# Two transformer blocks on one core: the compression product of block one with high and low inputs side by side, and its output product placed behind the first attention score

## The reference, cut to what matters

```python
def compress(kv, pe, w1, w2):
    """Overlapping blocks (length CMP_BLOCK, stride CMP_STRIDE) -> one token via MLP with intra-block pos. emb."""
    B, G, T, dh = kv.shape
    NC = (T - CMP_BLOCK) // CMP_STRIDE + 1
    idx = jnp.arange(NC)[:, None] * CMP_STRIDE + jnp.arange(CMP_BLOCK)[None, :]
    blocks = kv[:, :, idx, :] + pe
    flat = blocks.reshape(B, G, NC, CMP_BLOCK * dh)
    return jax.nn.silu(flat @ w1) @ w2
...
        kc = rmsnorm(compress(heads(kcm, KVH), cmp_pe[i, 0], cmp_w1[i, 0], cmp_w2[i, 0]), nsa_knorm_g[i, 0])
        vc = compress(heads(vcm, KVH), cmp_pe[i, 1], cmp_w1[i, 1], cmp_w2[i, 1])
        s_cmp = jnp.einsum('bgntd,bgcd->bgntc', q_nope, kc) * scale
        p_cmp = masked_softmax(s_cmp, cmp_mask)
        o_cmp = jnp.einsum('bgntc,bgcd->bgntd', p_cmp.astype(vc.dtype), vc)
```

## Time and profile before

| what | value |
|---|---|
| median of 3 runs | 2827.45 us (2824.11 to 2828.16) |
| span of the profiled execution | 2822.0 us |
| between the span and the median of the runs | 5.45 us |
| PE busy | 2731.9 us, 97% of the span |
| DVE, ACT, POOL busy | 1176.7, 1271.7, 1385.1 us |
| mean granted TensorE clock | 0.991 |
| PE of the chain that ended last | 87% |

### The profile page before, as it was taken

The page is one execution under the profiler, slowest core; times in us unless marked ns, Lnnn a source line. Parts: engine busy times, 40 slices in busy tenths (PEclk is TensorE's granted clock), DMA queues, the critical chain, the costliest instruction groups (busy, mean ns, idle before and its releaser), DMA issues.

```text
span 2822.0 us, 41633 instructions
## 1 busy us (share of the span) xinstructions
PE 2731.9 (97%) x13748; PEld 2286.9 (81%) x13748; DVE 1176.7 (42%) x2138; ACT 1271.7 (45%) x2187; POOL 1385.1 (49%) x1713
## 2 busy tenths in 40 slices
PE   8999899999999999999999999999999999999998
PEld 6889668788867878888888888888888788888887
DVE  4768752567775234422242321313442324242232
ACT  5554745655564543545443432424344544343233
POOL 4535444543544454454643655545455464365553
PEclk9999999999899999999999999999999999999999
DMA  5223113322301242233432333334223342233332
GB/s 152 72 51 87 26 31 90 87 72 57 92 9 45 83 113 70 83 102 100 120 98 60 110 100 90 97 97 114 70 82 101 96 125 90 65 107 102 93 97 97
DMA packets 270820, 242.47 MB, mean 86 GB/s; under 512 B 29376, under 2 KB 203648, under 8 KB 270592
## 3 DMA queue, kind: packets, MB, share of 16 engines
q1 hardware_dynamic: 267696, 235.12, 28.7%
q10 hardware_dynamic: 2896, 4.52, 0.5%
HBM read 237.51 MB, written 2.10 MB: 85 GB/s over the span
## 4 chain that ended last, share of the span: by engine, by line
PE 87%; DVE 5%; issue 4%; ACT 3%; POOL 0%; DMA 0%; DVEq 0%; ACTq 0%; POOLq 0%
PE bank L1988 11%; PE bank L1992 11%; PE bank L1991 11%; PE bank L1922 8%; PE bank L1925 8%; PE bank L1926 8%; PE bank L841 5%; PE bank L845 4%; PE bank L844 4%; PE bank L979 2%; PE bank L1877 2%; PE bank L891 1%; PE bank L827 1%; PE bank L894 1%; PE bank L895 1%
## 5 line engine op out<-in xcount | busy, mean ns | idle before, releaser
L2832 POOL TENSOR_TENSOR wlo<-raw,whi 128x256 fp32r<-128x256 f32 (+1 forms) x1616 | 1290.1, 830 | 1302.8 <-ACT whi L2137 1302.5
L2137 ACT CAST whi<-raw 128x1024 fp32r<-128x1024 f32 (+2 forms) x443 | 455.5, 1034 | 598.6 <-PE bank L1988 401.9
L1922 PE MATMUL bank<-xhi,whi 128*128 128x512 f32 x928 | 363.9, 392 | 1.6 <-DVE h L2524 1.6
L1926 PE MATMUL bank<-xhi,wlo 128*128 128x512 f32 x928 | 361.3, 389 | 0.0
L1925 PE MATMUL bank<-xlo,whi 128*128 128x512 f32 x928 | 361.1, 389 | 0.0
L1988 PE MATMUL bank<-whi,xhi 128*128 128x512 f32 x832 | 326.5, 392 | 3.9 <-DVE xlo L2415 3.9
L1992 PE MATMUL bank<-whi,xlo 128*128 128x512 f32 x832 | 324.0, 389 | 0.0
L1991 PE MATMUL bank<-wlo,xhi 128*128 128x512 f32 x832 | 323.8, 389 | 0.0
L841 PE MATMUL bank<-whi,xhi 128*128 128x512 f32 (+2 forms) x672 | 246.6, 367 | 5.5 <-DVE pT L1497 3.1
L844 PE MATMUL bank<-wlo,xhi 128*128 128x512 f32 (+2 forms) x672 | 242.2, 360 | 0.0
L845 PE MATMUL bank<-whi,xlo 128*128 128x512 f32 (+2 forms) x672 | 242.1, 360 | 0.0
(11 more groups left out here) (509 smaller groups left out, 4954.4 us busy)
## 6 DMA issues: line engine op xcount, KB each, us to landing
raw<-in_w_in SPq DMA_DIRECT2D x147, 512.0 KB, 3.7
raw<-in_w SPq DMA_DIRECT2D x132, 512.0 KB, 3.8
raw<-in_w_pg SPq DMA_DIRECT2D x16, 512.0 KB, 3.8
raw<-in_w_o SPq DMA_DIRECT2D x16, 512.0 KB, 3.8
raw<-in_xa_k SPq DMA_DIRECT2D x16, 512.0 KB, 3.9
raw<-in_xa_v SPq DMA_DIRECT2D x16, 512.0 KB, 3.8
raw<-in_xa_q SPq DMA_DIRECT2D x16, 512.0 KB, 4.0
raw<-in_xa_o SPq DMA_DIRECT2D x16, 512.0 KB, 3.8
```

The lines of the kernel that those rows point to most:

```text
L1922: mm = pe.matmul(o, wh, rhs[0][:, k, :], start=(k == 0), stop=False)
L1926: mm = pe.matmul(o, wl, rhs[0][:, k, :], start=False, stop=(k == KD - 1))
L2137: nc.scalar.copy(whi[:, j % SLOTS, 0:nk * cols], raw[:, j % SLOTS, 0:nk * cols]).then_inc(hi_split, 1)
L2832: ins = nc.gpsimd.tensor_tensor(wlo[:, s, part], raw[:, s, part], whi[:, s, part].bitcast(F32), ALU.subtract)
```

## The change

The input of `c_hid` lies as one tensor `chl`, with high and low parts next to each other. One matmul of 124 columns does `whi` by both, and one of 62 columns does `wlo` by the high part: two matmuls in place of three. The two halves of the bank are added by a new DVE reduction to `hsum`, which empties the bank; ACT's sigmoid and DVE's product read `hsum` in place of the bank. In the order, `score 0` and `fill 0` now come first, `c_out` behind them, `nz_exp 1` behind `c_out`, then (by place in the list) `exp 0`, `score 1`, `nz_gate 1`, `fill 1`, `c_key`, `c_score 0`, `score 2`.

```diff
-    s += [("nz_exp", 1), ("c_out",), ("nz_gate", 1)]
     main, last = attention_steps()
-    main.insert(1, ("c_key",))
+    first = [("score", 0), ("fill", 0, FILL[0]), ("c_out",), ("nz_exp", 1)]
+    assert main[:2] == [("score", 0), ("c_score", 0)]
+    main[:2] = first
+    place(main, ("score", 1), [("nz_gate", 1), ("fill", 1), ("c_key",), ("c_score", 0)])
...
-    place(main, ("score", 0), [("fill", 0, FILL[0])], ahead=True)
-    place(main, ("score", 2), [("fill", 1)])
...
+        hsum = Ql[:, 0, 128:128 + 4 * NCMP].rearrange("p (w c) -> p w c", w=2)
...
-            chi0, clo0 = (sb(n, [P, 16, 2, NCMP], F32R, middle) for n in ("chi0", "clo0"))
+            chl0 = sb("chl0", [P, 16, 2, 2 * NCMP], F32R, middle)
...
-                o = G.ps(name)[:, 0:2 * NCMP]
+                both, high = G.ps(name)[:, 0:4 * NCMP], G.ps(name)[:, 0:2 * NCMP]
                 for j in range(8):
-                    a, b = (x[:, 8 * i + j].rearrange("p g c -> p (g c)") for x in ((chi0, clo0), (chi1, clo1))[w])
+                    x = (chl0, chl1)[w][:, 8 * i + j]
                     wh, wl = whi[:, s, j * P:(j + 1) * P], wlo[:, s, j * P:(j + 1) * P]
-                    mm = pe.matmul(o, wh, a, start=(i == 0 and j == 0), stop=False)
+                    mm = pe.matmul(both, wh, x.rearrange("p a c -> p (a c)"), start=(i == 0 and j == 0), stop=False)
                     if j == 0:
                         mm.then_inc(chunk_begun, 1)
-                    pe.matmul(o, wh, b, start=False, stop=False)
-                    mm = pe.matmul(o, wl, a, start=False, stop=(i == 1 and j == 7))
+                    mm = pe.matmul(high, wl, x[:, 0], start=False, stop=(i == 1 and j == 7))
...
             def step_c_hid(step):
                 if step[2] == 1:
-                    gate(("ch", step[1]), 2 * NCMP)
+                    gate(("ch", step[1]), 2 * NCMP, src=hsum[:, step[1], :])
...
             def step_c_hid(step):
                 if step[2] == 1:
-                    name = ("ch", step[1])
+                    name, w = ("ch", step[1]), step[1]
+                    dve.wait_ge(*G.filled(name, l))
+                    nc.vector.tensor_reduce(hsum[:, w, :], G.ps(name)[:, 0:4 * NCMP].rearrange("p (a c) -> p c a", a=2), AX, ALU.add).then_inc(*G.empty(name))
+                    dve.wait_ge(*G.evacuated(name, l))
                     e = et_place()[:, 0:2 * NCMP]
-                    tt_(hid[:, step[1], :], e, G.ps(name)[:, 0:2 * NCMP], ALU.mult).then_inc(*G.empty(name))
+                    tt_(hid[:, w, :], e, hsum[:, w, :], ALU.mult).then_inc(*et_read[0].up())
```

More of the change, by code:

```diff
@@ L587, in build @@
         fa, fb, fc, ft = (tA[:, :], et[:, 0, :]), (tB[:, :], sq[:, 0, :]), (tC[:, :], sq[:, 1, :]), (Ql[:, 0, :], Ql[:, 1, :])
-        chi1 = nc.alloc_sbuf_tensor_at("chi1", [P, 16, 2, NCMP], F32R, offset=decays_at)
-        clo1 = nc.alloc_sbuf_tensor_at("clo1", [P, 16, 2, NCMP], F32R, offset=decays_at + 16 * 2 * NCMP * 4)
+        chl1 = nc.alloc_sbuf_tensor_at("chl1", [P, 16, 2, 2 * NCMP], F32R, offset=decays_at)
         kdt = tC[:, :].rearrange("p (c d) -> p c d", c=TT)
@@ L1061, in step_c_out @@
             def step_c_out(step):
-                for w in range(2):
-                    pe.wait_ge(*G.evacuated(("ch", w), l))
+                gated = [s_ for s_ in steps1[:steps1.index(step)] if s_[0] in ("z_gate", "nz_gate") or s_[0] == "c_hid" and s_[2] == 1]
+                pe.wait_ge(*et_read[0].at(l, len(gated)))
                 pe.wait_ge(*G.free(("co",), l))
@@ L1399, in step_c_in @@
                 act.wait_ge(*G.evacuated(("ct", w, 1), l))
-                nc.scalar.copy((chi0, chi1)[w][:, :, :, :], cin).then_inc(*sigs["hi"].up())
+                nc.scalar.copy((chl0, chl1)[w][:, :, 0, :], cin.rearrange("p j g c -> p j (g c)")).then_inc(*sigs["hi"].up())
             def step_c_hid(step):
                 if step[2] == 1:
-                    gate(("ch", step[1]), 2 * NCMP)
+                    gate(("ch", step[1]), 2 * NCMP, src=hsum[:, step[1], :])
             def step_c_out(step):
@@ L1427, in step_c_turn @@
                 if qt == 0:
-                    act.wait_ge(*et_read[0].at(l, 2 * TT))
+                    act.wait_ge(*et_read[0].at(l, 2 * TT + 2))
                 for g in range(NKV):
@@ L1763, in step_c_in @@
                 dve.wait_ge(*hi_s.next(l))
-                tt_((clo0, clo1)[w][:, :, :, :].rearrange("p j g c -> p (j g c)"), cin.rearrange("p j g c -> p (j g c)"),
-                    (chi0, chi1)[w][:, :, :, :].rearrange("p j g c -> p (j g c)").bitcast(F32), ALU.subtract).then_inc(*clo_ready.up())
+                x = (chl0, chl1)[w]
+                tt_(x[:, :, 1, :], cin.rearrange("p j g c -> p j (g c)"), x[:, :, 0, :].bitcast(F32), ALU.subtract).then_inc(*clo_ready.up())
             def step_c_hid(step):
                 if step[2] == 1:
-                    name = ("ch", step[1])
+                    name, w = ("ch", step[1]), step[1]
+                    dve.wait_ge(*G.filled(name, l))
+                    nc.vector.tensor_reduce(hsum[:, w, :], G.ps(name)[:, 0:4 * NCMP].rearrange("p (a c) -> p c a", a=2), AX, ALU.add).then_inc(*G.empty(name))
+                    dve.wait_ge(*G.evacuated(name, l))
                     e = et_place()[:, 0:2 * NCMP]
-                    tt_(hid[:, step[1], :], e, G.ps(name)[:, 0:2 * NCMP], ALU.mult).then_inc(*G.empty(name))
+                    tt_(hid[:, w, :], e, hsum[:, w, :], ALU.mult).then_inc(*et_read[0].up())
             def step_c_out(step):
```

## The result

The changed kernel takes 2843.22 us (median of 4 runs, 2842.61 to 2845.74), the kernel before on the same chip 2827.8 us (4 runs, 2824.11 to 2829.63). The ratio is 1.0055, with a 95% interval of 1.0043 to 1.0067: 15.4 us slower. That is inside the forecast range of 2832 to 2848 and on the forecast side, 3.7 us above the likeliest value.

A forecast was written before the change was run, and what follows sets the result against it. PE was taken as 87% of the chain, with the attention behind the key copies. Copies later by 5.8 and 6.2 us gave +12.0: span 2822.0 to 2834, median 2827.45 to 2839.5 us, range 2832 to 2848.

The forecast's parts named there:

- The product: Compression product: 64 matmuls a layer instead of 96 save 3.8 us of PE work, all hidden in a wait for DVE.
- rival A: Compression product: the PE work saved reaches the end, with both stalls gone; -12.6 us, 2815; chance 5%.
- The reductions: DVE behind the query rotation: two a layer at 0.28 us, delaying ACT's sigmoids; the subtractions still end at 289.84.
- the cover: ACT's 1.52 us wait for PE before the `qhl` casts hides the sigmoid delay; if gone, up to 1.4 us a layer.
- The stall ahead of the output product: PE after the compression product: `score 0` needs only the last `qhl`, so PE resumes 0.75 and 0.4 us earlier.
- What is late next: `c_out` behind `score 0` and `fill 0` ends at 296.4 in layer one; key copies 6.5 us later, near 302.9.
- The bank: `score 1` shares bank 5 with `c_out` and waits for DVE to read it; worth 1.7 us a layer.
- Rival B: Attention slack absorbs ACT's lateness, so only the stall's 0.75 + 0.4 us are gained; 2826; chance 7%.
- The term that was mis-sized: Second layer's key copies: 780.1 + 6.5 = 786.6 against 780.42, so +6.2 us.
- rival D: Clock falls again behind the new waits, so `score 1` and `fill 1` cost 3.0 us more a layer; +18, 2845; 18%.
- The step from span to time: Whole kernel: the runs' median 2827.45 lies 5.45 us above the profiled span, so span 2834 becomes 2839.5.
- the +12.0: Both layers together: key copies +5.8 us in the first and +6.2 us in the second.

The follow-up runs named there:

- experiment 3: The run of co_bank7: changed kernel with `c_out` in bank 7, `c_key` in 6, `p_turn` in 7 and 4; 2838.09 us.
- order_only: Kernel before with only the lines of the change that set the order, keeping its three-matmul product; 2841.14 us, ratio 1.0047 to before.
- fill1_later: Changed kernel with `fill 1` put back behind `score 2`; 2839.84 us, ratio 1.0041 to the kernel before.
- co_bank7: Changed kernel with `c_out` in bank 7, `c_key` in bank 6, `p_turn` in 7 and 4, set by hand; 2838.09 us, ratio 1.0036 to before.
- co_then_fill: Changed kernel with `c_out` right behind `score 0` and `fill 0` behind it; 2835.86 us, ratio 1.0026 to the kernel before.

## Why the prediction was right, and where a size was off

**The product: right.** I said that PE would be done with the `kk` transposes near 276.8 and wait some 2.7 us for bank 0 behind DVE's rotation; it waits 2.43 and, in the second layer, 5.70. Alone, the product doesn't make the kernel faster (1.0007), which rules out rival A.

**The reductions: right.** Priced at 0.28, they take 0.27 and 0.29. The subtractions `qhl` began at 283.83 and ended at 289.49 (I said 289.84, unchanged). ACT's wait of 1.52 us for PE in the earlier trace rows was the cover, and 0.29 of it is left (283.22).

**The stall ahead of the output product: right in the first layer.** `score 0` at 289.64, forecast 289.9. In the second layer I said 0.4 us gained; there it is a small loss. The rows of DVE's gate product ahead of the stretch, before and changed:

```profile
755.02 0.68 DVE L1606 TENSOR_TENSOR nzs<-nzs,et 128x512 f32<-128x512 f32 x1
```

```profile
760.88 0.68 DVE L1605 TENSOR_TENSOR nzs<-nzs,et 128x512 f32<-128x512 f32 x1
```

The layer starts 5.86 us late. Less that, `score 0` is at 773.24 against the forecast of 772.5, since PE's transposes of `q` ran at the lower clock and ACT had to wait 0.90 us for them; DVE's subtractions began at 773.29 - 5.86 = 767.43, not at 766.8.

**What is late next: right, link by link.** `c_out` ends at 295.9 (forecast 296.4); the wait for bank 5 is 2.12 (2.06); the key copies come at 302.40 (302.9), `exp 1` 5.38 us later (5.26), the wait ahead of `score 4` is 3.14 (some 3). The bank was priced at 1.7 us a layer; experiment 3 gives 1.6 up to the key copies where the clock is the same. That bears out the rule of the Trainium skill that I set against the trace there (Perfetto Trace Analysis, Matmuls: independent groups should rotate through banks): with both groups in bank 5 PE waited 2.12 us in both layers, and with `c_out` in bank 7 it didn't wait. Rival B, that the attention absorbs the delay, is out: the 5.45 us at `exp 1` are the same 5.45 at 322.81.

**The term that was mis-sized** is the second layer, "second layer 780.1 + 6.5 = 786.6 against 780.42: +6.2". It measures 796.04 - 5.86 = 790.18, +9.76. Of the 3.56 us more, 2.99 are `score 1` and `fill 1` at the lower level (7.05 - 4.06). The rest is about what `c_out` ended later than forecast (786.56 - 5.86 = 780.70 against 780.1), from the late `score 0`. Those 2.99 are rival D's 3.0 a layer, in one layer of two. So one term was off, the clock behind the wait, and that the number came as near as it did is in part luck: it happened once and not twice.

In every trace of the second layer that has the wait of 2.12 us (changed, order_only, fill1_later), PE ran at the lower level behind it; in the two kernels with the same product and no wait (co_bank7, co_then_fill) the clock was 1.00 from 788 to 796. In order_only it ran low only from 791.67 to 795.1, and `score 1` and `fill 1` took 5.63 us (791.38 to 797.01), 1.6 more than in its first layer and not 3.0. In the first layer of these three kernels the full clock stayed behind the same wait. Why stays open. PE had run at the full level for 2.3 us ahead of the wait in the changed kernel's first layer (from 293.65), and for only 1.4 us in the second (from 785.13); for 2.6 and 1.0 us in order_only, 2.0 and 1.6 us in fill1_later. No run changed that alone.

**The step from span to time** did no harm. The profiled execution of before was some 3.6 us faster than the median, but as the +12.0 is in the end added to the median of 2827.45, the forecast doesn't move. As a difference of medians it was +12.0 and the result +15.4. In the key copies the first layer gave 0.5 less than I said (5.33 against 5.8) and the second 3.6 more, together 3.1 of the missing 3.4 us.

## What to carry to other kernels

Work saved on an engine that next waits for another one's long operation is only a longer wait: look up what releases the next step before pricing the matmuls. When steps change places in a queue, ask for each moved step what stands right behind it and whether that needs its output bank, and price the gap twice: its own length, and PE's work behind it at half the clock. A short step at the head of a long chain (here the compressed key, whose copies set `exp 1`) was best placed ahead of the filling work, and filling work in the gap behind it. Once it was early enough, the next engine in the chain, here DVE, held things: `exp 1` 2.3 us earlier brought 0.8 us behind the first layer's stretch (layer 1, -0.79), and the second layer added no gain (+0.02).

## What the runs showed of the hardware that I had not expected

A matmul of 124 columns and one of 62 beside it took 0.22 us together at the full clock, and 0.43 at the lower level. By their starts that is 0.14 and 0.08, on average 0.11, the same as for the 62-column matmuls of the kernel before (0.11 from start to start, 0.21 at the lower level). So in this form the 62 columns more had no price in the pair that shows, and at the same clock 64 matmuls instead of 96 did cut PE's time for the product by a third.

```profile
268.22 0.31 PE L1053 MATMUL bank<-chl,whi 128*128 128x124 f32 x1
268.36 0.25 PE L1056 MATMUL bank<-chl,wlo 128*128 128x62 f32 x1
268.44 0.30 PE L1053 MATMUL bank<-chl,whi 128*128 128x124 f32 x1
```

The same pause of 2.12 us was followed by full clock in one layer and by 0.57 in the other. So a gap's cost to the clock isn't a fixed sum; for the same 33 matmuls behind it, it was 0 us (changed and order_only, first layer), 1.6 (order_only, second) or 3.0 (changed, second).
